# Storing finished output rows by row number while the last expert tile is still loading

## The chip, the cores and the metric

The program runs on one core of a Trainium2 chip. A core has a matrix engine (TensorE, PE in the profile), a vector engine (VectorE, DVE), an activation engine (ScalarE, ACT), a general engine (GpSimd, POOL) and a queue engine (SyncE, SP) that here only issues DMAs. Sixteen DMA engines move data between the chip's DRAM and the core's on-chip memory; the profile shows them by queue: q1 holds what SP issues, q10 what ACT issues, q0 what POOL issues. The metric is the time of one execution in microseconds on the device; less is better.

## The reference, cut to what matters

One decoder layer on 512 tokens of width 2048: three token mixers, then a mixture of experts, then a final normalisation. The change lies wholly in the last two. The last lines are

```python
# hier_moe: every token goes to 2 of 32 experts (top group, then top 2 in the group)
h = jax.nn.silu(lax.ragged_dot(xs, w_gate, sizes)) * lax.ragged_dot(xs, w_up, sizes)
y = lax.ragged_dot(h, w_down, sizes)
y = y * gates_flat[order][:, None]
out = jnp.zeros_like(xt).at[token_of].add(y)
# after it: residual add, then one last RMSNorm with gain final_norm_g
y = xf * lax.rsqrt(jnp.mean(xf * xf, axis=-1, keepdims=True) + EPS) * g
```

An output row is therefore finished once both experts of its token have been added. A row that no expert of the last tile touches is finished before the last tile is.

## The kernel before

**Tiles.** The tokens are sorted by expert and packed into 14 tiles of 128 places (`NTILE`, tiles 0 to 13; `LAST` is 13). The last tile holds four experts with 32 places each (`OWNERS`, `FOUR`). The kernel's second half is a loop over these tiles: a tile's rows are gathered from DRAM (`hs_d`) by POOL with an indirect DMA (L880), turned over by PE, multiplied by the gate and up weights (L1319), joined by ScalarE (silu) and VectorE, turned over again, and multiplied by the down weights. What comes out (`YSB`, one row for each place) is added to the rows of the residual `H0`, which holds all 512 rows as four blocks of 128 rows by 2048 columns. Adding is done by PE with a selection matrix `SEL` (POOL, L891): row t of a block picks the place that holds it, scaled by its gate; VectorE adds the product to `H0` (`combined`, L1774).

**Weights.** SP loads every expert's weights in order into eight slots and waits for a slot to be free before each load. For the last tile the gate and up weights come as four halves, each 4 x 2 MB, and the down weights as six pieces of columns (`DOWN_PIECES`: 512, 512 and four times 256 columns, each for four experts, issued at L744 and L746). Pieces 0 and 1 go into slots that the third half frees, pieces 2 to 5 into slots that the fourth frees. Nothing else is loaded after piece 5.

**The last tile.** `last_tile` on PE runs `first_products`, which goes through the four halves and calls `ahead(half)` before each: it fills PE's time while that half loads. In it stand what is left of adding tile 12 (`combine`) and, before the fourth half, the spreading of the final gain over the partitions. After the hidden values, six pieces follow (`y_part`, L1428: the down products of one piece; then `combine_part`, L1440: four selection products, one for each block of rows). ScalarE or VectorE copies each piece to `YSB` between the two. VectorE adds each product to `H0` (`add`), ScalarE squares it and sums (`square`), VectorE multiplies by the gain (`times_g`). After the last piece each block gets its sum, root and inverse (`sum_of`, `std`, `inverse_of`) and is scaled, blocks 0 and 2 on VectorE and 1 and 3 on ScalarE (`scaled`). SP stores each block in two halves (L750) and waits for all eight stores.

The order on every engine is written out by hand and held by semaphores; no scheduler moves anything.

Of the kernel before, what the change touches and what calls it, by code (L numbers as in the profile page):

```python
# [8 lines left out]
ALU = mybir.AluOpType  # L9
ACT = mybir.ActivationFunctionType  # L10
AX = mybir.AxisListType
# [90 lines left out]
def build(nc, d, out, cc):  # L102

    ctx = ExitStack()
    with ctx:
# [160 lines left out]
        FG, HG3, PART = XG[0], XT, TOT  # L266
# [173 lines left out]
        for at_, s in enumerate(steps):  # L440
# [50 lines left out]
        disc_act, disc_dve, disc_done = sem("disc_act"), sem("disc_dve"), sem("disc_done")  # L491
# [31 lines left out]
        g_done, out_dve, out_act, out_done = (  # L523
            sem("g_done"), sem("out_dve"), sem("out_act"), sem("out_done"))
# [7 lines left out]
        Y_BANK, Y_ACT = (4, 5, 6, 7, 4, 5), (True, False, True, False, True, False)  # L532
        Y_COPIES = [sum(Y_ACT[i] == Y_ACT[p] for i in range(p + 1)) for p in range(NPC)]

# [115 lines left out]
        def _(sp):  # L650
# [105 lines left out]
        def _(pool):  # L756
# [149 lines left out]
            with pool.If(flag > 0):  # L906
# [22 lines left out]
                pool.wait_ge(o_sel, NOV + 2)  # L929
            pool.wait_ge(sel_ready, LAST)  # L930
            selection(LAST)
# [3 lines left out]
        def _(pe):  # L935
# [58 lines left out]
            def do(s):  # L994
# [84 lines left out]
                elif kind == "ab":  # L1079
                    once(disc_done, 1)  # L1080
# [318 lines left out]
            def last_tile(n, parts):  # L1399

                def ahead(half):
                    for t in ((0, 1), (2,), (3,), ())[half]:
                        combine(n - 1, t)
                    if half == 3:
                        pe.wait_ge(fg_in, 16)
                        pe.wait_ge(comb_done, 16 * n + 1)
                        for q in range(4):
                            mm(B(4 + q, [(1, 512)]), F(C["ones"], P, 0, 1), F(FG + q * 512, 512, 0, 1), start=True,
                               stop=True).then_inc(fg_spread, 1)

# [3 lines left out]
                pe.wait_ge(fg_done, 4)  # L1414

                def y_part(p):
# [7 lines left out]
                    if p >= 4:  # L1424
                        pe.wait_ge(y_act if Y_ACT[p - 4] else y_dve, 2 * n + 1 + Y_COPIES[p - 4])
# [6 lines left out]
                def combine_part(p):  # L1432
                    lo, cols = PIECES[p][:2]
                    pe.wait_ge(y_act if Y_ACT[p] else y_dve, 2 * n + 1 + Y_COPIES[p])
                    if p == 0:
                        pe.wait_ge(sel_ready, n + 1)
                    for t in range(TB):
                        if p:
                            pe.wait_ge(comb_done, 16 * n + 4 * (p - 1) + t + 2)
                        mm(B(t, [(1, cols)]), F(SEL + t * P, P), F(YSB + lo, cols), start=True,  # L1440
                           stop=True).then_inc(comb_full, 1)

                for p in range(NPC):
                    y_part(p)
                    combine_part(p)
# [34 lines left out]
        def _(act):  # L1480
# [233 lines left out]
            def square(t, p):  # L1714
                lo, cols = PIECES[p][:2]
                act.wait_ge(comb_done, 16 * LAST + 4 * p + t + 2)
                A(F(SIL, cols), F(H0 + t * D + lo, cols), ACT.Square,
                  accum_out=F(PART + NPC * t + p, 1)).then_inc(squares_done, 1)
                act.wait_ge(squares_done, SQ0 + 4 * p + t + 1)

            def y_copy_last(p):
                lo, cols = PIECES[p][:2]
                act.wait_ge(y_full, 2 * LAST + p + 1)
                A(F(YSB + lo, cols), B(Y_BANK[p], [(1, cols)]), ACT.Copy).then_inc(y_act, 1)

            y_copy_last(0)
            A(F(SSQ, 1), F(EPSC, 1), ACT.Sqrt)
            for p in range(NPC - 1):
# [871 lines left out]
```

## Time and profile before

| | us |
|---|---|
| time before, median of 3 runs (lowest, highest) | 1947.87 (1946.85, 1950.14) |
| span of the profiled execution, first to last instruction | 1943.8 |
| median less that span: what lies around the instructions | 4.1 |
| last half of the gate and up weights: PE starts, ends | 1883.3, 1892.6 |
| first down product | 1894.9 |
| last down piece: PE starts | 1924.6 |
| first store of output issued | 1930.7 |

The profiled execution's own time is not given apart from its span; the median is 4.1 us longer than the span, and the two are taken to differ by that much.

The page of the profile gives busy shares over the whole span: PE 92%, VectorE 41%, ScalarE 13%, POOL 9%. From the twentieth slice on the DMA engines are 97 to 100% busy at some 425 GB/s: the expert loop runs at the pace of the weights. Only the last slice differs, with 7 tenths and 279 GB/s. What the change does all happens in the last 90 us, so the views are read for that stretch: the windows (busy time of each engine, clock and DMA share of a stretch), the timeline of one engine (start, duration, and in brackets the idle time before and what ended it), the DMA view of a window, and the chain that ended last.

### The profile page before, as it was taken

How to read it: one execution, taken by the hardware profiler on the slowest of the kernel's cores; microseconds unless marked ns; L12 is line 12 of the kernel's file. 1: busy time of each engine (PE TensorE's matmuls, PEld its weight loads, DVE VectorE, ACT ScalarE, POOL GpSimd, SP SyncE). 2: the span in 40 equal slices, each digit the busy share in tenths (PEclk: the TensorE clock that was granted, in tenths of full speed). 3: DMA queues.
4: the chain of work that ended last, by engine and by line, in shares of the span. 5: the costliest groups of instructions: out<-in, count | busy, mean ns of one | idle time of the engine just before them, and what ended most of it. 6: DMA issues, size and time to landing. Idle time of an engine off the chain costs nothing.

```text
span 1943.8 us, 30977 instructions
## 1 busy us (share of the span) xinstructions
PE 1792.7 (92%) x13019; PEld 1147.0 (59%) x13019; DVE 792.5 (41%) x1533; ACT 248.9 (13%) x588; POOL 173.5 (9%) x200
## 2 busy tenths in 40 slices
PE   6999999999999989999796679999999999999766
PEld 4888899889998879999642223332333333333222
DVE  7666684367467554333421112331222222222205
ACT  3012111200224431000210000000000000000004
POOL 1443342000000000000010000000000000000000
PEclk9999999999999999999898789999999999999988
DMA  6343333312121242422699999999999999999997
GB/s 220 98 139 88 99 88 90 101 63 66 52 85 55 71 170 66 173 67 66 275 378 425 426 427 425 426 426 425 422 425 422 423 425 426 425 424 423 416 413 279
DMA packets 68089, 506.12 MB, mean 260 GB/s; under 512 B 18824, under 2 KB 18972, under 8 KB 40872
## 3 DMA queue, kind: packets, MB, share of 16 engines
q1 hardware_dynamic: 50546, 480.40, 61.2%
q0 software_dynamic: 5008, 15.35, 2.4%
q10 hardware_dynamic: 12400, 8.36, 1.7%
q8 instruction: 109, 1.79, 0.4%
q14 instruction: 26, 0.21, 0.0%
HBM read 497.28 MB, written 12.99 MB: 263 GB/s over the span
## 4 chain that ended last, share of the span: by engine, by line
PE 69%; DMA 24%; DVE 3%; ACT 2%; issue 1%; SPq 1%; ACTq 0%; DVEq 0%
PE psum L986 20%; DMA arena<-in_moe_w_gate 17%; PE psum L1319 17%; PE psum L989 16%; PE psum L1278 5%; DMA arena<-in_moe_w_up 3%; DMA arena<-in_moe_w_down 3%; PE psum L1356 2%; PE psum L1144 2%; DVE arena L1774 1%; PE psum L1045 1%; PE psum L1428 1%; DVE arena L1777 1%; PE psum L1175 1%; PE psum L1440 1%
## 5 line engine op out<-in xcount | busy, mean ns | idle before, releaser
L1319 PE MATMUL psum<-arena 128*32 128x512 f32 x3584 | 417.4, 620 | 70.6 <-DMA arena<-in_moe_w_gate 38.0
L986 PE MATMUL psum<-arena 128*128 128x128 f32 x3584 | 410.7, 276 | 0.0
L986 PEld LDWEIGHTS psum<-arena 128*128 128x128 f32 x3584 | 405.3, 193 | 7.1 <-issue 6.4
L1774 DVE TENSOR_TENSOR arena<-psum,arena 128x512 f32<-128x512 f32 (+1 forms) x323 | 212.4, 674 | 403.2 <-PE psum L1278 374.3
L1319 PEld LDWEIGHTS psum<-arena 128*32 128x32 f32 x3584 | 119.4, 114 | 360.3 <-issue 349.6
L989 PE MATMUL psum<-arena 128*128 128x256 f32 x1456 | 322.4, 380 | 1.1 <-DVE arena L1774 1.1
L989 PEld LDWEIGHTS psum<-arena 128*128 128x128 f32 x1456 | 273.8, 190 | 38.7 <-issue 2.1
L1774 DVE TENSOR_TENSOR arena<-arena,psum 128x256 f32<-128x256 f32 (+2 forms) x172 | 75.1, 437 | 449.5 <-PE psum L986 215.6
L1774 DVE TENSOR_TENSOR arena<-arena 128x256 f32<-128x256 f32 (+17 forms) x474 | 191.2, 445 | 33.2 <-ACT arena L1486 25.3
L1356 PE MATMUL psum<-arena 128*32 128x512 f32 x1664 | 185.1, 603 | 17.9 <-DMA arena<-in_moe_w_down 17.9
L1278 PE MATMUL psum<-arena 128*128 128x512 f32 x416 | 192.1, 605 | 1.2 <-DVE arena L2417 1.2
L583 DVE TENSOR_TENSOR arena<-arena 128x1024 f32<-128x1024 f32 x116 | 149.0, 1285 | 3.2 <-DVE arena L1774 1.8
L1278 PEld LDWEIGHTS psum<-arena 128*128 128x128 f32 x416 | 74.9, 190 | 119.0 <-issue 119.0
L1356 PEld LDWEIGHTS psum<-arena 128*32 128x32 f32 x1664 | 54.2, 111 | 139.4 <-issue 138.4
L891 POOL TENSOR_SCALAR arena<-arena 128x512 f32<-128x512 f32 x14 | 29.1, 2080 | 788.1 <-PE psum L1278 787.7
L1551 ACT ACTIVATE arena<-psum 128x256 f32<-128x256 f32 x50 | 19.0, 381 | 291.8 <-PE psum L989 201.1
L1678 ACT ACTIVATE arena<-psum 128x512 f32<-128x512 f32 x14 | 8.4, 597 | 359.6 <-PE psum L1299 359.6
L1674 ACT ACTIVATE arena<-psum 128x512 f32<-128x512 f32 x14 | 8.4, 597 | 342.2 <-PE psum L1319 342.2
L2417 DVE COPY arena<-psum 128x512 f32<-128x512 f32 x13 | 9.0, 691 | 94.8 <-PE psum L1356 94.8
L2414 DVE COPY arena<-psum 128x512 f32<-128x512 f32 x13 | 9.0, 691 | 87.6 <-PE psum L1356 87.6
L1486 ACT ACTIVATE arena<-psum 128x512 f32<-128x512 f32 (+3 forms) x65 | 29.9, 484 | 92.4 <-PE psum L1133 25.1
L1634 ACT ACTIVATE arena<-arena 128x128 f32<-128x128 f32 (+3 forms) x48 | 26.6, 554 | 89.8 <-DVE arena L1777 89.7
(216 smaller groups left out, 1033.3 us busy)
## 6 DMA issues: line engine op xcount, KB each, us to landing
arena<-in_moe_w_gate SPq DMA_DIRECT2D x64, 2048.0 KB, 26.9
arena<-in_moe_w_up SPq DMA_DIRECT2D x64, 2048.0 KB, 25.0
arena<-in_moe_w_down SPq DMA_DIRECT2D x56, 2048.0 KB, 27.1
arena<-in_w_in SPq DMA_DIRECT2D x86, 512.0 KB, 4.6
arena<-in_w_out SPq DMA_DIRECT2D x32, 512.0 KB, 4.9
arena<-in_x SPq DMA_DIRECT2D x8, 1024.0 KB, 8.3
arena<-in_moe_w_down SPq DMA_DIRECT2D x8, 1024.0 KB, 18.2
arena<-in_moe_w_down SPq DMA_DIRECT2D x16, 512.0 KB, 12.1
```

The costliest lines, as they stand in the source:

```text
L583: e.tensor_tensor(F(o, BLK), F(a, BLK), F(b, BLK), ALU.subtract).then_inc(sums_ready, 1)
L891: g.tensor_scalar(F(SEL, S), F(IOTA, S), F(SELP, 1), F(SELP + 1, 1), ALU.is_equal, ALU.mult).then_inc(sel_ready, 1)
L986: last = mm(B(bank, [(1, P)], off=t * P), F(a + t * P, P), F(w + i * P, P), start=start and t == 0, stop=(i == KH - 1), skip_group_check=True)
L989: last = mm(B(bank, [(1, HB)]), F(w + i * P, P), F(a, HB), start=start, stop=(i == KH - 1), skip_group_check=True)
L1045: last = mm(B(bank, [(1, S)]), F(w + k * P, P), F(ZT + k * S, S), start=(k == 0), stop=(k == NB5 - 1))
L1144: last = mm(B(bank, [(1, P)], off=t * P), F(KT + h * S + t * P, P), F(QT + h * S + t * P, P), start=True, stop=True)
L1278: mm(B(4 + q, [(1, 512)]), F(SEL + t * P, P), F(YSB + q * 512, 512), start=True, stop=True).then_inc(comb_full, 1)
L1319: last = mm(B(bank, [(1, FE)], 32 * g, 32), F(xt + c * CAP + 32 * g, 32), F(SLOT[slot] + (c % 8) * FE, FE), start=(c == 0), stop=(c == KD ...
L1356: last = mm(B(4 + q, [(1, 512)], 32 * g, 32), F(HTE + m * CAP + 32 * g, 32), down_block(slot, m, q), start=(m == 0), stop=(m == FT2 - 1))
L1486: A(dst, B(bank, dims[0], *dims[1:]), func, **kw).then_inc(free[bank], 1)
L1634: last = A(x, x, ACT.Exp, bias=F(SM + (u % 2) * 8 + m, 1), accum_out=F(SM + (u % 2) * 8 + 2 + m, 1))
L1774: return v.tensor_tensor(o, a, b, op)
```

## The change

- **Early rows.** After tile 12 has been added, ScalarE squares and sums all of `H0` (four operations of 2048 columns), and VectorE scales the four blocks in place by the inverse root and the gain (four operations of 2048 columns).
- **Stores by row number.** POOL stores each block with an indirect DMA whose row numbers (`BIDX`) are the block's own rows, but out of bounds for rows that the last tile holds; those are not written. They are issued as soon as a block is scaled.
- **The last tile in its own rows.** PE gathers the raw `H0` rows of the last tile's 128 places into four PSUM banks with one-hot products (16 products of 512 columns, `ahead(3)`), before `H0` is scaled. A matrix `SAME` (places that hold the same token, scaled by their gate) takes the place of the four selection products: one product for a piece, added onto those banks. The norm is then worked out on 128 rows and not on 512, and one indirect DMA stores them by their token numbers.
- **Moved.** Tile 12's blocks 2 and 3 are both added before the second half, and the spreading of the gain moves from before the fourth half to before the third, with four turn-overs of the one-hot matrix (`OHS` to `OHT`) and one product for `SAME`.
- SP issues no store any more and waits for the five indirect ones. Down products use PSUM banks 0 and 1 in turn.
- `disc_done` is replaced by a count of `disc_dve`, far ahead in the program.

```diff
@@ sync
-            for t in range(TB):
-                for half in range(2):
-                    sp.wait_ge((out_dve, out_act)[t % 2], 3 * (t // 2) + 1 + 2 * half)
-                    sp.dma_start(DV(out, t * P * D + half * (D // 2), [(D, P), (1, D // 2)]),
-                                 F(H0 + t * D + half * (D // 2), D // 2)).then_inc(out_done, 16)
-            sp.wait_ge(out_done, 2 * 16 * TB)
+            sp.wait_ge(out_done, 16 * (TB + 1))
@@ gpsimd
-            selection(LAST)
+            pool.wait_ge(xT_full, 4 * LAST + 4)
+            g.tensor_copy(F(SELP, 1), TOKC[:, LAST:LAST + 1]).then_inc(sel_col, 1)
+            g.tensor_copy(F(SELP + 1, 1), GSLC[:, LAST:LAST + 1]).then_inc(sel_col, 1)
+            pool.wait_ge(sel_col, 2 * LAST + 2)
+            g.tensor_scalar(F(OHS, S), F(IOTA, S), F(SELP, 1), 1.0, ALU.is_equal, ALU.mult).then_inc(sel_ready, 1)
+            g.tensor_scalar(F(TOKD, P), F(IDENT, P), F(SELP, 1), 1.0, ALU.mult, ALU.mult).then_inc(sel_ready, 1)
+            def to_rows(src, idx):
+                g.indirect_dma_start(out=out[:, :], out_offset=bass.IndirectOffsetOnAxis(ap=idx, axis=0),
+                                     in_=F(src, D), in_offset=None, bounds_check=S - 1,
+                                     oob_is_err=False).then_inc(out_done, 16)
+            for t in range(TB):
+                pool.wait_ge(same_ready, t + 3)
+                to_rows(H0 + t * D, F(BIDX + t, 1).bitcast(U32))
+            pool.wait_ge(out_dve, 2)
+            pool.wait_ge(out_act, 1)
+            to_rows(HGS, TOKV[:, LAST:LAST + 1])
@@ tensor, last_tile
-                    for t in ((0, 1), (2,), (3,), ())[half]:
+                    for t in ((0, 1), (2, 3), (), ())[half]:
                         combine(n - 1, t)
-                    if half == 3:
+                    if half == 2:
+                        pe.wait_ge(sel_ready, n + 2)
+                        for t in range(TB):
+                            last = tr(B(0, [(1, P)], off=t * P), F(OHS + t * P, P), ident)
+                        last.then_inc(same_full, 1)
+                        mm(B(1, [(1, P)]), F(C["ones"], P), F(TOKD, P), start=True, stop=True).then_inc(same_full, 1)
                         ...
+                    elif half == 3:
+                        pe.wait_ge(same_ready, 1)
+                        for q in range(4):
+                            pe.wait_ge(fg_done, q + 1)
+                            for t in range(TB):
+                                last = mm(B(4 + q, [(1, 512)]), F(OHT + t * P, P), F(H0 + t * D + q * 512, 512),
+                                          start=(t == 0), stop=(t == TB - 1), skip_group_check=True)
+                        last.then_inc(same_full, 1)
-                def combine_part(p):
+                def same_part(p):
                     ...
+                    mm(final_bank(p), F(SAME, P), F(YSB + lo, cols), start=False, stop=True,
+                       skip_group_check=True).then_inc(comb_full, 1)
@@ scalar
+                for t in range(TB):
+                    A(F(YSB, D), F(H0 + t * D, D), ACT.Square, accum_out=F(SSQ + t, 1)).then_inc(squares_done, 1)
+                    act.wait_ge(squares_done, SQ0 + t + 1)
+                A(F(STD, TB), F(SSQ, TB), ACT.Sqrt, scale=1.0 / D, bias=F(EPSC, 1)).then_inc(h_std, 1)
             ...
+            for p, (lo, cols, *_) in enumerate(PIECES):
+                ...
+                act.wait_ge(comb_full, 16 * LAST + p + 2)
+                A(F(SIL, cols), final_bank(p), ACT.Square, accum_out=F(PART + p, 1)).then_inc(squares_done, 1)
+            ...
+            A(F(SSTD, 1), F(SSUM, 1), ACT.Sqrt, scale=1.0 / D, bias=F(EPSC, 1)).then_inc(h_std, 1)
+            ...
+            A(F(HGS + D // 2, lo - D // 2), F(HGS + D // 2, lo - D // 2), ACT.Copy, scale=F(SRST, 1)).then_inc(out_act, 1)
@@ vector
+            dve.wait_ge(h_std, 2)
+            v.reciprocal(F(RST, TB), F(STD, TB)).then_inc(h_rst, 1)
+            dve.wait_ge(h_rst, 2)
+            dve.wait_ge(fg_done, 4)
+            dve.wait_ge(same_full, 3)
+            for t in range(TB):
+                h = F(H0 + t * D, D)
+                v.scalar_tensor_tensor(h, h, F(RST + t, 1), F(FG, D), M, M).then_inc(same_ready, 1)
             hidden_dve(LAST, ends(last_parts())[1])
             ...
+                if p < LASTP:
+                    dve.wait_ge(squares_done, SQ0 + TB + p + 1)
+                    tt(F(HGS + lo, cols), final_bank(p), F(FG + lo, cols), M).then_inc(comb_done, 1)
             ...
+            ts(F(HGS, D // 2), F(HGS, D // 2), F(SRST, 1), None, M).then_inc(out_dve, 1)
+            v.scalar_tensor_tensor(F(HGS + lo, cols), final_bank(LASTP), F(SRST, 1), F(FG + lo, cols), M,
+                                   M).then_inc(out_dve, 1)
```

On TensorE, from the last half's products to the second down piece, the program before reads as follows (L1319 up products, L1299 turn-overs of the hidden values, L1428 down products, L1440 selection products):

```order
L1319 MATMUL psum<-arena 32x512 [waits slot_in4,slot_in1,slot_in6,slot_in3]
L1319 MATMUL psum<-arena 32x512 x31
L1299 MATMUL psum<-arena 128x128 [waits h_done]
L1299 MATMUL psum<-arena 128x128 x3
L1428 MATMUL psum<-arena 32x512 [waits slot_in7,slot_in2,slot_in5,slot_in0,fg_done,hT_done]
L1428 MATMUL psum<-arena 32x512 x15
L1440 MATMUL psum<-arena 128x512 [waits sel_ready,y_act]
L1440 MATMUL psum<-arena 128x512 x3
L1428 MATMUL psum<-arena 32x512 [waits tail_in1]
L1428 MATMUL psum<-arena 32x512 x15
```

The same place in the changed program, from the last of the gathering products (new L1440) on; L1339, L1319, L1458 and L1469 are up products, turn-overs, down products and `SAME` products:

```order
L1440 MATMUL psum<-arena 128x512 [waits fg_done]
L1440 MATMUL psum<-arena 128x512 x3
L1339 MATMUL psum<-arena 32x512 [waits slot_in4,slot_in1,slot_in6,slot_in3]
L1339 MATMUL psum<-arena 32x512 x31
L1319 MATMUL psum<-arena 128x128 [waits h_done]
L1319 MATMUL psum<-arena 128x128 x3
L1458 MATMUL psum<-arena 32x512 [waits slot_in2,slot_in7,slot_in0,slot_in5,hT_done]
L1458 MATMUL psum<-arena 32x512 x15
L1469 MATMUL psum<-arena 128x512 [waits same_ready,y_act]
L1458 MATMUL psum<-arena 32x512 [waits tail_in1]
```

Sixteen gathering products now stand ahead of the last half, and after each down piece one product stands where four stood.

On VectorE, from the adding of tile 12 on, the program before reads as follows (the second row is the hidden product of the last tile, the third and fourth are the additions of piece 0, the last its multiplications by the gain):

```order
L1774 TENSOR_TENSOR arena<-psum,arena 128x512 [waits comb_full] x16
L1774 TENSOR_TENSOR arena<-arena,psum 128x512 [waits silu_done,slot_used1]
L1774 TENSOR_TENSOR arena<-psum,arena 128x512 [waits comb_full,fg_done]
L1774 TENSOR_TENSOR arena<-psum,arena 128x512 [waits comb_full] x3
L1774 TENSOR_TENSOR arena<-arena 128x512 [waits squares_done] x4
```

The same place in the changed program (L2471 scales the early rows, the L1778 behind it is the hidden product):

```order
L1778 TENSOR_TENSOR arena<-psum,arena 128x512 [waits comb_full] x16
L2457 COPY arena<-psum 128x512 [waits same_full]
L1781 TENSOR_SCALAR arena<-psum,arena 128x128 [waits same_full]
L2461 TENSOR_REDUCE arena<-arena 128x4 [waits same_ready]
L2462 SCALAR_TENSOR_TENSOR arena<-arena 128x4 [waits dve_step]
L2463 CAST arena<-arena 128x4 [waits dve_step]
L2465 RECIPROCAL arena<-arena 128x4 [waits h_std,dve_step]
L2471 SCALAR_TENSOR_TENSOR arena<-arena 128x2048 [waits same_full,fg_done,h_rst]
L2471 SCALAR_TENSOR_TENSOR arena<-arena 128x2048 x3
L1778 TENSOR_TENSOR arena<-arena,psum 128x512 [waits silu_done,slot_used1]
```

The hidden product of the last tile waits behind the four scalings, and these wait for the last gathering product.

## Rows read from the trace of the kernel before

**Rows 1.** Span and mean granted TensorE clock of the core.
```profile
core 0: 1943.8 us, clock 0.969
```

**Rows 2.** Windows of 1889 to 1923 us: stretch, length, busy by engine, PEclk, DMA share, GB/s.
```profile
1889.00:1903.00 14.00, 11.63 (x80) 3.75 (x72) 2.81 (x5) 4.24 (x9) 0.00 (x0) 1.00 1.01 406
1903.00:1916.00 13.00, 11.41 (x88) 4.95 (x92) 10.36 (x18) 5.58 (x17) 0.00 (x0) 1.00 1.02 404
1916.00:1923.00 7.00, 5.89 (x74) 3.47 (x67) 5.10 (x14) 3.49 (x14) 0.00 (x0) 1.00 0.35 140
```

**Rows 3.** Timeline of SP, last weight load and last store; start, duration.
```profile
1908.07 0.93 SPq L746 DMA_DIRECT2D arena<-in_moe_w_down  x1
...
1938.70 1.13 SPq L750 DMA_DIRECT2D out<-arena  x1
```

**Rows 4.** DMA view of 1908.0 to 1908.2: that load; last number us to landing.
```profile
arena<-in_moe_w_down SPq DMA_DIRECT2D x1, 512.0 KB, 15.4
```

**Rows 5.** Timelines of PE and ACT, last tile; start, duration, records, idle before.
```profile
1863.71 8.87 PE L1319 MATMUL psum<-arena 128*32 128x512 f32 x64 [7.54 <-DMA arena<-in_moe_w_up]
1872.52 3.70 PE L1408 MATMUL psum<-arena 1*128 1x512 f32 x8
...
1873.67 0.60 ACT L1710 ACTIVATE arena<-psum 128x512 f32<-128x512 f32 x1 [20.39 <-PE psum L1408]
...
1883.34 9.30 PE L1319 MATMUL psum<-arena 128*32 128x512 f32 x64 [7.13 <-DMA arena<-in_moe_w_up]
1894.86 3.64 PE L1428 MATMUL psum<-arena 128*32 128x512 f32 x32 [0.69 <-ACT arena L1678]
...
1924.55 1.93 PE L1428 MATMUL psum<-arena 128*32 128x256 f32 x32
```

**Rows 6.** The chain that ended last, from the last piece; start, duration, engine and line.
```profile
1926.55 0.44 DVE arena L2469
...
1927.03 0.71 PE psum L1440 x2
...
1928.35 0.32 ACT arena L1717
...
1928.68 0.19 ACT arena L1717
...
1929.43 0.30 ACT arena L1736
...
1929.76 0.17 DVE arena L2492
```

**Rows 7.** Groups of instructions, 1889 to 1944: busy us, mean ns of one.
```profile
L1777 DVE TENSOR_SCALAR arena<-arena 128x1024 f32<-128x1024 f32 (+1 forms) x4 | 2.6, 684 | 0.1
L2500 DVE SCALAR_TENSOR_TENSOR arena<-arena 128x256 f32<-128x256 f32 x2 | 1.0, 480 | 0.0
```

**Rows 8.** Timeline of VectorE: four multiplications by the gain, 2048 columns in all.
```profile
1903.56 2.49 DVE L1774 TENSOR_TENSOR arena<-arena 128x512 f32<-128x512 f32 x4
```

**Rows 9.** Timeline of POOL: the gather for the last tile.
```profile
1681.04 1.09 POOL L880 DMA_INDIRECT arena<-hs_rows,arena  x1 [0.87 <-POOL arena L877]
```

**Rows 10.** DMA view of 1681.0 to 1684.7: queues with packets, MB, share; that gather.
```profile
q1 hardware_dynamic: 109, 1.59, 101.1%
...
arena<-hs_rows,arena POOLq DMA_INDIRECT x1, 12.7
```

**Rows 11.** DMA view of 1684.7 to 1692.3: packets, MB, share of each queue.
```profile
q1 hardware_dynamic: 203, 2.95, 92.2%
q0 software_dynamic: 142, 0.25, 8.6%
```

**Rows 12.** DMA view of the page: sizes in KB, median us to landing.
```profile
arena<-y_scratch POOLq DMA_DIRECT2D x5, 256.0 KB, 3.0
```

**Rows 13.** DMA view of 1939.2 to 1944: the last store of the output.
```profile
out<-arena SPq DMA_DIRECT2D x1, 512.0 KB, 4.7
```

**Rows 14.** DMA view of 988 to 991, weights beside stores of hidden rows (q10).
```profile
DMA packets 108, 1.28 MB, mean 426 GB/s; under 512 B 1, under 2 KB 1, under 8 KB 1
```

More of the change, by code:

```diff
@@ L265, in build @@
         SEL, SELP = SIL + 4 * CAP, SIL + 4 * CAP + S
-        FG, HG3, PART = XG[0], XT, TOT
+        FG, HGS, PART = XG[0], XT, TOT
+        OHS, OHT, SAME, TOKD, BIDX = XG[1], XG[1] + S, XG[1] + 2 * S, XG[1] + 2 * S + P, XG[1] + 2 * S + 2 * P
+        SSUM, SSTD, SRST, HASL = SM + 1, SM + 2, SM + 3, SM + 4
         assert RO2 == RO1 + 128
@@ L1079, in do @@
                 elif kind == "ab":
-                    once(disc_done, 1)
+                    once(disc_dve, 3)
                     for i, r in enumerate((10, 11, 14, 15)):
@@ L1435, in combine_part @@
                     if p == 0:
[L1436 to L1441, printed above, removed]
+                        pe.wait_ge(same_ready, 2)
+                    if lo % 512:
+                        pe.wait_ge(comb_done, 16 * n + p + 1)
+                    mm(final_bank(p), F(SAME, P), F(YSB + lo, cols), start=False, stop=True,
+                       skip_group_check=True).then_inc(comb_full, 1)
                 for p in range(NPC):
                     y_part(p)
-                    combine_part(p)
+                    same_part(p)
             expert_tile(0, 0, 0, fixed_parts(), THREE_ONE, True)
@@ L1721, in y_copy_last @@
[L1721 to L1728, printed above, removed]
-                if p and Y_ACT[p]:
-                    y_copy_last(p)
-                for t in range(TB):
-                    square(t, p)
-            def std(t):
-                act.wait_ge(squares_sum, t + 2)
-                A(F(STD + t, 1), F(SSQ + t, 1), ACT.Sqrt, scale=1.0 / D, bias=F(EPSC, 1)).then_inc(h_std, 1)
@@ L1746, in _ @@
[L1746 to L1755 removed]
+            for p, (lo, cols, *_) in enumerate(PIECES):
+                if Y_ACT[p]:
+                    act.wait_ge(y_full, 2 * LAST + p + 1)
+                    A(F(YSB + lo, cols), B(Y_BANK[p], [(1, cols)]), ACT.Copy).then_inc(y_act, 1)
+                act.wait_ge(comb_full, 16 * LAST + p + 2)
+                A(F(SIL, cols), final_bank(p), ACT.Square, accum_out=F(PART + p, 1)).then_inc(squares_done, 1)
+                act.wait_ge(squares_done, SQ0 + TB + p + 1)
@@ L2466, in y_copy @@
-            def y_copy(p):
-                lo, cols = PIECES[p][:2]
-                dve.wait_ge(y_full, 2 * LAST + p + 1)
-                v.tensor_copy(F(YSB + lo, cols), B(Y_BANK[p], [(1, cols)])).then_inc(y_dve, 1)
-            dve.wait_ge(fg_done, 4)
-            for p in range(LASTP):
-                if not Y_ACT[p]:
-                    y_copy(p)
-                for t in range(TB):
-                    add(t, p)
-                if p < LASTP - 1:
-                    for t in range(TB):
-                        times_g(t, p)
@@ L2508, in _ @@
-            settle()
-            add(0, LASTP)
-            add(1, LASTP)
-            sum_of(0)
-            last_g(1)
-            add(2, LASTP)
-            inverse_of(0)
-            scaled(0)
-            sum_of(1)
-            add(3, LASTP)
-            inverse_of(1)
-            sum_of(2)
-            last_g(3)
-            inverse_of(2)
-            sum_of(3)
-            inverse_of(3)
-            scaled(2)
+            dve.wait_ge(same_full, 1)
+            v.tensor_copy(F(OHT, S), B(0, [(1, S)])).then_inc(same_ready, 1)
@@ new lines, in _ @@
+            dve.wait_ge(same_full, 2)
+            ts(F(SAME, P), B(1, [(1, P)]), F(SELP, 1), F(SELP + 1, 1), ALU.is_equal, M).then_inc(same_ready, 1)
+            dve.wait_ge(same_ready, 2)
+            settle(v.tensor_reduce(F(HASL, TB), V(OHT, [(P, TB), (1, P)]), AX.X, ALU.max))
+            settle(v.scalar_tensor_tensor(F(HASL, TB), F(HASL, TB), SENT, F(C["tok"], TB), M, AD))
+            settle(v.tensor_copy(F(BIDX, TB).bitcast(U32), F(HASL, TB)))
+            dve.wait_ge(h_std, 2)
+            v.reciprocal(F(RST, TB), F(STD, TB)).then_inc(h_rst, 1)
```

86 lines of the change are left out of this document (22 added, 64 removed).

## The prediction

> **What bounds the kernel now.** I read the windows of the last weights first. From 1889 to 1916 us the DMA share is 1.01 and 1.02, at 406 and 404 GB/s; from 1916 to 1923 it falls to 0.35 [rows 2]. So up to the last weights the stretch belongs to the DMA engines. A share of 0.35 over 7 us means that some of the sixteen engines work longer than the others, and that weights land until the slowest is through: the last load is issued at 1908.07 [rows 3] and lands 15.4 us later [rows 4], at 1923.5. TensorE is next: its clock is 1.00 all along [rows 2], its first down product starts at 1894.86 and the last piece at 1924.55, 1.1 us after its weights are there [rows 5]. TensorE's and the DMA's ends thus nearly coincide. The chain then runs through copy, selection product, square, root and scaling to the last store, issued at 1938.70 [rows 3] and landed 4.7 us later [rows 13], at 1943.4; the span ends at 1943.8 [rows 1], 0.4 us behind.
>
> From the landing of the last weights to the end it is 20.3 us. The change attacks these, and in return puts stores into the stretch where the DMA engines have no idle time. That exchange is the whole question.
>
> **Change, part 1: the early stores among the weights.** The gather for the last tile shows how many rows that tile holds: in its stretch queue q0 moved 0.25 MB [rows 11], and a row is 8 KB, so some 30 rows. The early stores leave these out and move 482 rows, 3.95 MB. They start when VectorE has scaled a block. The sixteen gathering products begin when the third half is done, at 1872.5; four products of 512 columns take 3.70 us there [rows 5], sixteen 14.7, to 1887.2. Each scaling has 2048 columns, which four multiplications of 512 did in 2.49 us [rows 8]; with fewer starts I take 2.25. The blocks are ready at 1889.5, 1891.7, 1894.0 and 1896.2.
>
> Are the stores served at once, or behind the weights? The gather put its 142 packets through in 7.6 us while q1 held 92% [rows 11]: q0 gets its turn beside a full q1. Four stores of 1 MB, issued by 1896.3 and moving from 3.7 us later (below), are through well before 1916. So all 3.95 MB pass ahead of the last weights, on engines that were never idle up to there. Stores and loads share one rate, they don't add: stores of hidden rows beside weights moved 426 GB/s together [rows 14]. At 426 GB/s the 3.95 MB take 9.3 us, at the 406 of this stretch [rows 2] 9.7. I take 9.4, since rows of 8 KB resemble the former. A lower bound: between 1916 and 1923 0.65 of the engines' time lies idle, 4.5 us; if the weights were dealt out so that this is used, the shift is 4.9. I don't take it, because the engine that ends last has its own share of the stores, and that isn't lent. The last weights land at 1923.5 + 9.4 = 1932.9.
>
> **Part 2: TensorE and VectorE ahead of the pieces.** The last half starts at 1887.2 instead of 1883.3 [rows 5]. Its 9.30 us held a slow start after 7.13 us of waiting; without that wait it should take 7 to 9.3, and ends at 1894.2 to 1896.5. The loads of pieces 2 to 5 wait for it, 2 to 4 us longer than before, while pieces 0 and 1 (8.4 MB issued, 20 us at the rate of rows 2) still fill the queue to past 1903. The hidden product on VectorE now stands behind the four scalings, until 1896.3; the first down product starts at about 1898.5 instead of 1894.86. From there TensorE alone would need, for pieces 0 and 1, 3.64 [rows 5] + 0.75 for the copy + 0.93 for one product, and for the other four 1.93 + 0.55 + 0.50 each: 10.6 + 11.9, to 1921. It is 12 us ahead of weights that land at 1932.9, so all of part 2 costs nothing; if the weights came unshifted, at 1923.5, it would still be hidden. For the same reason the 18 selection products that go gain nothing by themselves; only the last piece's count, in part 3. The four squares and the copies of the gain lie where ScalarE waited 20.39 us [rows 5]; a copy of 512 columns took 0.60 there, so a square of 2048 takes at most 2.4, and all four some 10. On TensorE the gain's spreading (3.70) changes places with the addition of block 3, as long as itself; only the turn-overs and the product for `SAME` are new before the third half, some 1 us, against 7.54 us of waiting [rows 5]. I cost all of it at nothing.
>
> **Part 3: from the last weights to the last store issued.** The same chain, one piece, one block [rows 6]: start of the piece to start of its copy 2.00, copy and hand-over 0.48 (next product at 1927.03), first product 0.80 with hand-over; then, without the addition to the residual, square 0.32 and its accumulator 0.19, with hand-overs 0.54; a reduction, taken as long as the reciprocal, 0.21; root 0.34; reciprocal 0.21; scaling 1024 columns 0.68 and 256 from PSUM 0.48 [rows 7], ScalarE's 768 columns beside them. Sum 5.7. The scaled rows stand at 1932.9 + 0.1 + 5.7 = 1938.7. Before, the last scaling and store issue were 15.2 us behind the weights; now 5.8. This is the gain: 9.4 us, and it happens to equal the shift of part 1.
>
> **Part 4: the last store.** Before it was a plain store of 512 KB by SP, 4.7 us with one before it in the queue [rows 13]. Now it is an indirect one by POOL. The gather is the nearest row: 0.87 us between the instruction ahead and its start [rows 9], 12.7 us from issue to landing, and no packet of q0 until 3.7 us after the issue [rows 10]; all packets lie within the next 7.6 us [rows 11], so 1.4 us are left for completion. These 3.7 + 1.4 = 5.1 are fixed. Without weights in the way the data take what the fullest engine has: eight rows of 8 KB at 426/16 GB/s, 2.5 us, even if the other engines are nearly empty. Landing after 7.6 us. The gap ahead I take as 0.6, between 0 and 0.87. Lower bound for the landing: POOL's plain loads of 256 KB landed in 3.0 [rows 12]. Upper: the gather's 12.7.
>
> The Trainium skill ("DMA: Bandwidth & Descriptors", section "Anatomy of one DMA — SWDGE (gpsimd) path") has another price for a DMA issued by POOL: about 2.0 us fixed plus the bytes at 436 GB/s. By it the last store, 0.25 MB, would take 2.6 us and the sum would come out 5.0 us lower. The gather's rows disagree: 3.7 us pass before the first packet alone. I go by the rows.
>
> **Sum.** 1938.7 + 0.6 + 7.6 + 0.4 = 1947.3 against 1943.8: 3.5 us longer. On the median of the runs shown that is 1947.87 + 3.5 = 1951.4, +0.18%. About 0.2% (3.9 us) is what a measurement of this kernel can tell from no change; the forecast is a loss just inside it. It comes from small terms: shift +9.4, chain -9.4, last store +3.5 (8.2 with its gap against 4.7).
>
> **Rivals.**
>
> *Slower: the mixed stretch runs below its rate.* Writes of rows to DRAM beside reads may cost more than 9.4 us for 3.95 MB. For it: the rate of this stretch is 405 and not 426 although the share is full [rows 2]. Against: rows 14. The outcome passes +0.2% once the shift is over 9.8 us, that is, when the stores run under 403 GB/s. At 340 GB/s it is 11.6 us and the time 1951.4 + 2.2 = 1953.6. An engine with no row left out carries 32 rows, 0.26 MB, at 405/16 GB/s 10.4 us: 1952.4.
>
> *Same, a little lower: idle engine time absorbs stores.* Shift 4.9 in place of 9.4: 1946.9. For it the 0.35 of rows 2, against it that the slowest engine carries its own part.
>
> *Faster: the last store is cheap as well.* If it lands in 3.0 us as POOL's plain loads do [rows 12], alone 1951.4 - 4.6 = 1946.8, no change that can be told; with the rival before it 1942.3.
>
> *Faster: the early stores wait.* If POOL's stores got little of the engines until the weights are through, the weights would land at 1923.5 and the last piece be ready at 1929.3; the stores would drain from 1923 to 1933 behind them and the last land at about 1936.5: 1943.8 - 6.9, a time of 1941.0. Then the change would do only half of what it says, and win by it. Against it: rows 11.
>
> **How the numbers follow.** The forecast's case (shift 9.3 to 9.8, last store 7 to 8 us) 0.42, most of it within 0.2%; slower by a lower rate, by a fuller engine or by a longer last store 0.38; absorbed or cheap store alone 0.10; both, or waiting stores 0.10. The sum lies near the bound, so I count 0.05 of the first case as slower: slower 0.43, same 0.47, faster 0.10. The likeliest is 1951.4, by itself 1950 to 1952. The range for 8 in 10: down to 1946.5, the absorbed case, and up to 1956, which is the 340 GB/s case with 2 us more for the last store.
>
> **What would show it.** Right: DMA share near 1 until about 1925 and the last weight landing at 1932 to 1934; TensorE waiting for DMA before most pieces; the last POOL store issued near 1939 to 1940 and landing some 8 us later; early stores done by 1916. Wrong in part 1 if the last weights land before 1930 or after 1935; in part 2 if TensorE starts the last piece more than 0.3 us after its weights; in part 4 if the last store takes under 6 or over 9 us.

## The result and the profile after

| | before | changed |
|---|---|---|
| median of 10 runs each, us | 1947.9 | 1951.43 |
| lowest, highest | 1945.7, 1950.14 | 1950.4, 1954.39 |
| span of the profiled execution | 1943.8 | 1949.2 |

The ratio of changed to before is 1.0019, 95% interval 1.0011 to 1.0027: 3.5 us longer. A second series of the same kernel, beside three of the experiments, gave 1951.94 against 1947.48, ratio 1.0023 (1.0014 to 1.0032), with a span of 1947.7. The two profiled executions differ by 5.4 us and not 3.5; 1.3 us of that difference is a delay in front of the change (TensorE ends the third half at 1873.8 and not 1872.5), which the second series' profile doesn't have: there TensorE ends it at 1872.3 and the span is 3.9 us longer. Nor do 4.1 us lie around the instructions, as was assumed for the kernel before: in every run on record with both numbers, a time is 1.8 to 3.1 us longer than its span, so the profiled execution before was a fast one. So all stretches below are counted from the end of the third half's products.

The windows of the changed kernel (stretch, length, busy time of PE, PEld, DVE, ACT and POOL, PEclk, DMA share, GB/s) answer to [rows 2]:

```profile
1889.00:1903.00 14.00, 10.38 (x84) 3.01 (x80) 8.64 (x5) 0.60 (x1) 7.08 (x4) 0.88 1.01 420
1903.00:1916.00 13.00, 6.47 (x38) 1.41 (x30) 0.69 (x1) 1.29 (x3) 0.00 (x0) 0.74 1.01 419
1916.00:1920.00 4.00, 3.18 (x30) 0.86 (x26) 0.69 (x1) 0.32 (x1) 0.00 (x0) 0.99 1.03 410
1920.00:1924.00 4.00, 2.14 (x30) 0.91 (x22) 1.12 (x2) 1.22 (x5) 0.00 (x0) 1.00 1.03 407
1924.00:1926.00 2.00, 1.70 (x32) 0.94 (x32) 0.00 (x0) 0.00 (x0) 0.00 (x0) 1.00 1.03 412
1926.00:1928.00 2.00, 0.93 (x9) 0.30 (x2) 0.42 (x1) 0.43 (x2) 0.00 (x0) 1.00 0.83 334
1928.00:1930.00 2.00, 0.61 (x11) 0.33 (x15) 0.42 (x1) 0.05 (x1) 0.00 (x0) 0.93 0.40 162
```

The full share reaches to 1926 where in the kernel before it ended at about 1916, at the same rate or a little more. Its TensorE timeline, from the gathering products (L1440) on, answers to [rows 5]; in brackets stands the idle time before and what ended it:

```profile
1873.76 14.00 PE L1440 MATMUL psum<-arena 128*128 128x512 f32 x32
1887.69 7.07 PE L1339 MATMUL psum<-arena 128*32 128x512 f32 x64
1897.70 0.66 PE L1319 MATMUL psum<-arena 128*128 128x128 f32 x4 [2.94 <-DVE arena L1778]
1899.04 5.29 PE L1458 MATMUL psum<-arena 128*32 128x512 f32 x32 [0.69 <-ACT arena L1707]
...
1911.99 5.64 PE L1458 MATMUL psum<-arena 128*32 128x512 f32 x32 [5.80 <-DMA arena<-in_moe_w_down]
...
1929.39 3.38 PE L1458 MATMUL psum<-arena 128*32 128x256 f32 x32 [1.92 <-DMA arena<-in_moe_w_down]
...
1934.46 1.93 PE L1458 MATMUL psum<-arena 128*32 128x256 f32 x32 [0.45 <-DMA arena<-in_moe_w_down]
```

Ahead of most pieces TensorE now waits for DMA, and it starts the last piece as the weights land; the kernel before started it 1.1 us after its weights. The end of the program stands in two views: POOL's timeline, and the source view of the closing instructions (minimum, median and maximum duration in ns, first and last start). A DRAIN is the instruction that closes an engine's program; SP's COMPARE_BRANCH is the first thing it does after its last wait, so its start tells when the last awaited transfer landed.

```profile
1891.14 2.31 POOL L942 DMA_INDIRECT out<-arena  x1 [85.99 <-DVE arena L2471]
1893.76 1.87 POOL L942 DMA_INDIRECT out<-arena  x1 [0.30 <-issue]
1895.94 1.94 POOL L942 DMA_INDIRECT out<-arena  x1 [0.30 <-issue]
1898.18 0.96 POOL L942 DMA_INDIRECT out<-arena  x1 [0.30 <-issue]
1940.97 0.96 POOL L942 DMA_INDIRECT out<-arena  x1 [41.83 <-DVE arena L2488]
```

```profile
L105 POOLq DRAIN  x1: 8208/8208/8208, 1940.8 to 1940.8; - x1
L105 SPq COMPARE_BRANCH  x1: 38/38/38, 1945.4 to 1945.4; - x1
```

The last store landed 4.4 us after its issue, at 1945.4, and SP, which waits for it, goes on at that moment. The program isn't over: POOL's closing DRAIN lasts 8.2 us and ends at 1949.0, 3.6 us behind the landing. What it follows, the experiments show. In the kernel before, the same instruction lay far from the end, and SP's last wait set it:

```profile
L105 POOLq DRAIN  x1: 8752/8752/8752, 1856.3 to 1856.3; - x1
...
L105 SPq COMPARE_BRANCH  x1: 37/37/37, 1943.4 to 1943.4; - x1
```

The difference of the two spans, in stretches:

| stretch | before | changed | difference |
|---|---|---|---|
| to the end of the third half | 1872.5 | 1873.8 | +1.3 |
| from there to the landing of the last weights | 51.0 (1923.5) | 60.6 (1934.4) | +9.6 |
| from there to the last scaled row or last store issue | 15.2 (1938.7) | 5.8 (1940.2) | -9.4 |
| from there to the end | 5.1 (1943.8) | 9.0 (1949.2) | +3.9 |

### The profile page after: what moved, and what is told of

Read it like the earlier page. It is cut to its first block, busy times and chain, and to the rows that moved or that the text cites. A ratio compares the mean times of both kernels' runs of the same rounds, so it can differ in the third digit from the quotient of the medians.

```text
span 1949.2 us, 30885 instructions
## 1 busy us (share of the span) xinstructions
PE 1801.3 (92%) x13021; PEld 1146.5 (59%) x13021; DVE 781.7 (40%) x1492; ACT 241.8 (12%) x552; POOL 181.7 (9%) x206
## 4 chain that ended last, share of the span: by engine, by line
PE 69%; DMA 22%; DVE 4%; SPq 2%; issue 1%; ACT 1%; POOLq 0%; DVEq 0%; POOL 0%; ACTq 0%
PE psum L1006 20%; PE psum L1339 16%; DMA arena<-in_moe_w_gate 16%; PE psum L1009 16%; PE psum L1298 5%; DMA arena<-in_moe_w_up 3%; PE psum L1376 3%; DMA arena<-in_moe_w_down 2%; PE psum L1164 2%; DVE arena L1778 2%; PE psum L1065 1%; SPq L753 1%; PE psum L1278 1%; PE psum L1440 1%; DMA arena<-hs_rows,arena 1%
## 5 line engine op out<-in xcount | busy, mean ns | idle before, releaser
L1339 PE MATMUL psum<-arena 128*32 128x512 f32 x3584 | 415.9, 618 | 56.8 <-DMA arena<-in_moe_w_gate 37.8
L1778 DVE TENSOR_TENSOR arena<-psum,arena 128x512 f32<-128x512 f32 x304 | 202.8, 684 | 394.8 <-PE psum L1298 356.5
L1339 PEld LDWEIGHTS psum<-arena 128*32 128x32 f32 x3584 | 118.4, 113 | 345.7 <-issue 327.7
L1778 DVE TENSOR_TENSOR arena<-arena,psum 128x256 f32<-128x256 f32 (+2 forms) x172 | 75.1, 437 | 411.9 <-PE psum L1006 215.6
L1778 DVE TENSOR_TENSOR arena<-arena 128x128 f32<-128x128 f32 (+17 forms) x452 | 181.0, 442 | 33.0 <-ACT arena L1515 25.1
```

The source lines that it names most:

```text
L1339: last = mm(B(bank, [(1, FE)], 32 * g, 32), F(xt + c * CAP + 32 * g, 32), F(SLOT[slot] + (c % 8) * FE, FE), start=(c == 0), stop=(c == KD ...
L1778: return v.tensor_tensor(o, a, b, op)
```

## Experiments

Ten kernels ran on the chip, each in five rounds beside the kernel before. A time is compared through its ratio to the kernel before in the same series; the intervals are about 0.09% to each side, 1.7 us, and 0.13% for the last kernel. Where a kernel stores fewer rows, SP's last wait counts fewer stores; that line isn't shown everywhere. Five kernels (no early stores, half of them, SP's plain stores with and without the wait for piece 4, the copy in place of the last store) leave rows of the output unwritten and serve only to tell causes apart.

### No early stores

```diff
-            for t in range(TB):
-                pool.wait_ge(same_ready, t + 3)
-                to_rows(H0 + t * D, F(BIDX + t, 1).bitcast(U32))
```

> Leaves out the four early stores, so that only the last tile's rows are written; all else as in the changed kernel. Theory A (stores and weights share one DMA rate): the last weights land 9.7 us earlier counted from the end of the third half's products, about 51 us behind them and not 60.6; time 1951.4 - 9.7 = 1941.7. Rival B (the later start of TensorE and VectorE delays the weights): they land 2 us earlier at most, time 1949 to 1951.

1943.49 us against 1947.65, ratio 0.9978 (0.9969 to 0.9987). Its TensorE timeline, third half's end and last piece:

```profile
1872.85 14.00 PE L1437 MATMUL psum<-arena 128*128 128x512 f32 x32
1886.78 7.07 PE L1336 MATMUL psum<-arena 128*32 128x512 f32 x64
...
1923.80 1.93 PE L1455 MATMUL psum<-arena 128*32 128x256 f32 x32 [0.41 <-DMA arena<-in_moe_w_down]
```

The last weights land at 1923.8, 50.9 us behind the third half, as in the kernel before. All that TensorE and VectorE do later in the changed kernel is still in it (sixteen gathering products, the last half at 1886.8), so none of this delays the weights: the 9.7 us come from the stores, and rival B falls. The time is 1.8 us above the 1941.7 expected: the medians give 8 us for the stores, the landings in the profiles 9.7.

### Half of the early stores

```diff
-            for t in range(TB):
+            for t in range(2):
                 pool.wait_ge(same_ready, t + 3)
```

> Only blocks 0 and 1 are stored early, blocks 2 and 3 not at all; all else as in the changed kernel. Theory A (each early byte delays the weights by its time at the common rate): half the bytes give half the shift, last weights 55.8 us behind the end of the third half's products, between 50.9 without early stores and 60.6 with all four; time midway between the two, about 1947. Rival F (idle engine time at the end absorbs the first few us of stores, about 4.5 us): the shift is near 0 to 1 us for two blocks, time 1943.5 to 1944.5.

1947.84 against 1947.48, ratio 1.0002 (0.9993 to 1.0011): in time midway, 4.1 us below the changed kernel of the same series (1951.94) and 4.4 above the one without early stores (of the other series). In the trace the weights land 54.5 us behind the third half (1874.6), a shift of 3.6 us and not 4.9:

```profile
1929.15 1.93 PE L1458 MATMUL psum<-arena 128*32 128x256 f32 x32 [0.56 <-DMA arena<-in_moe_w_down]
```

The engine that ends last counts, and its share of the rows in each block isn't shown; that may be why half the stores gave a third of the shift. Rival F (the first few us are free) fails: 3.6 us isn't near 0 to 1.

### Early stores after the last weights

```diff
+            pool.wait_ge(tail_in[5], 4 * 16)
             for t in range(TB):
                 pool.wait_ge(same_ready, t + 3)
```

> The early stores wait until the last piece of weights has landed (one more wait on POOL ahead of them). Theory A: weights land as in the kernel before, the stores' 9.5 us run beside the last chain (5.8 us) and beside what POOL needs at the end; the end is the last weights + 5.8 + 2 + 8.2 = 16 us behind the weights, against 20.3 before: 1943.5. Rival C (the bytes cost the same wherever they stand): 1951, since the same bytes then stand behind the weights. Rival B: 1951, nothing changes.

1946.64 against 1947.65, ratio 0.9994 (0.9985 to 1.0003). Slower than expected by 3 us, but some 5 us faster than the changed kernel, which rules out rival C. The weights land 51.4 us behind the third half, 0.5 more than without early stores although no early store had begun: half a microsecond is the scatter of these landings, and the shift in the changed kernel is 9.2 to 9.7 us. What I had missed stands in the closing instructions:

```profile
L105 POOLq DRAIN  x1: 11662/11662/11662, 1932.5 to 1932.5; - x1
L105 SPq COMPARE_BRANCH  x1: 38/38/38, 1940.6 to 1940.6; - x1
```

The stores land at 1940.6, because they started only at 1926, and POOL's DRAIN ends 3.6 us behind that, at 1944.2. Its windows show what lay idle before:

```profile
1920.00:1924.00 4.00, 3.31 (x32) 1.39 (x32) 0.00 (x0) 0.36 (x1) 0.00 (x0) 0.62 0.25 99
1924.00:1928.00 4.00, 2.63 (x34) 1.24 (x34) 0.42 (x1) 0.50 (x3) 1.59 (x2) 1.00 0.10 39
```

### Early stores after piece 4, and after piece 3

```diff
-            pool.wait_ge(tail_in[5], 4 * 16)
+            pool.wait_ge(tail_in[4], 4 * 16)
```

> The early stores wait for piece 4 of the weights instead of piece 5. In the run that waited for piece 5 the DMA engines were busy 0.25 and 0.10 of 1920 to 1928, and POOL's DRAIN ended 3.6 us behind the landing of the stores at 1940.6. Theory A+D: stores start 5 us earlier in idle time, land before the floor of last POOL instruction + 7 us, and the end falls by 3 us against that run, to 1943.5; the weights land up to 1 us later. Rival F: the weights still land unshifted. Rival G (stores delay the slowest engine by their full time wherever they start before its end): weights 3 us or more later and no gain.

1942.97 against 1947.48, ratio 0.9978 (0.9969 to 0.9987): 4.5 us faster than the kernel before, 9.0 faster than the changed kernel in the same series. All outputs are stored. TensorE's last piece, POOL's timeline and the windows:

```profile
1925.12 1.93 PE L1459 MATMUL psum<-arena 128*32 128x256 f32 x32 [0.47 <-DMA arena<-in_moe_w_down]
```

```profile
1920.87 1.07 POOL L942 DMA_INDIRECT out<-arena  x1 [115.55 <-DMA arena<-in_moe_w_down]
...
1931.62 0.96 POOL L942 DMA_INDIRECT out<-arena  x1 [5.86 <-DVE arena L2489]
```

```profile
1920.00:1924.00 4.00, 3.39 (x33) 1.44 (x33) 0.00 (x0) 0.38 (x1) 2.52 (x3) 0.63 0.56 228
1924.00:1928.00 4.00, 2.98 (x36) 1.48 (x36) 0.85 (x2) 0.47 (x2) 1.46 (x2) 1.00 0.99 402
1928.00:1932.00 4.00, 0.30 (x2) 0.00 (x0) 1.47 (x4) 1.70 (x4) 0.38 (x1) 0.72 1.00 412
1932.00:1936.00 4.00, 0.00 (x0) 0.00 (x0) 0.00 (x0) 0.00 (x0) 0.59 (x1) 0.50 0.30 117
```

The stores fill 1923 to 1933. The last weights land at 1925.1, 51.4 us behind the third half, 0.4 later than without early stores and no later than in the kernel that waits for piece 5, so rival G fails; 0.4 us is too little to tell theory A from rival F here. The stores' first packets came between 1922.3 and 1922.6, 2.8 us ahead of that landing, and until 1923.5 the weights kept a share of 0.23 to 0.27 of the engines, as without stores; why the stores took so little from them isn't shown. All stores have landed at 1936.1, the DRAIN ends at 1939.6, 7.0 us behind POOL's last instruction.

The same with one piece less to wait for:

```diff
-            pool.wait_ge(tail_in[5], 4 * 16)
+            pool.wait_ge(tail_in[3], 4 * 16)
```

> The early stores wait for piece 3. They then start at about 1918 to 1919, when four engines still carry weights for 5 us. Theory A: on these the stores take half the turns, weights 2 to 5 us later, time 1945 to 1948, above the kernel that waits for piece 4. Rival F: idle engine time takes them, weights unshifted, time 1943 or less.

1952.64 against 1947.48, ratio 1.0026 (1.0017 to 1.0036), 9.7 us slower than the wait for piece 4. Counted from the third half the stores are issued 5.0 us earlier, and the last weights now pay for nearly all of them, as the last piece on TensorE shows:

```profile
1932.06 3.35 PE L1459 MATMUL psum<-arena 128*32 128x256 f32 x32 [8.98 <-DMA arena<-in_moe_w_down]
```

The last weights land at 1932.0, 59.9 us behind the third half (1872.2), a shift of 9.0. That is nearly the full price, though the mean share of the engines in the stretch was far under 1 (0.20 from 1928 to 1932). The piece itself took 3.35 us at the low clock and not 1.93. Rival F fails, and my bound for theory A (2 to 5 us later) was too low. One part of that is plain: the first packets of the stores came between 1916 and 1917, 44 us behind the third half, so that weights which land at 51 without stores had some 7 us to go, and not 5. The other is how two queues share an engine. The DMA view of 1918 to 1922 (packets, MB, share of each queue; q0 is POOL's, q1 the weights'):

```profile
q0 software_dynamic: 214, 1.49, 88.6%
q1 hardware_dynamic: 57, 0.20, 12.2%
```

In the kernel that waits for piece 5 the last weights alone moved some 28 packets in each us, a share of about 0.25; here they got half of that, 57 packets in 4 us. A packet of q0 carried 7.0 KB on the average and one of q1 3.5, so turns in equal number would favour the stores; that this is the reason isn't shown.

### What the last store costs: another queue, and a copy in its place

The last rows by SP to a scratch tensor, so that the output lacks them:

```diff
-            pool.wait_ge(out_dve, 2)
-            pool.wait_ge(out_act, 1)
-            to_rows(HGS, TOKV[:, LAST:LAST + 1])
@@ sync
+            for half in range(2):
+                sp.wait_ge(out_dve, 1 + half)
+                ...
+                sp.dma_start(DV(hs_d, half * (D // 2), [(D, P), (1, D // 2)]),
+                             F(HGS + half * (D // 2), D // 2)).then_inc(fg_in, 16)
+            sp.wait_ge(fg_in, 48)
+            sp.wait_ge(out_done, 16 * TB)
```

> The last tile's rows are stored by SP with two plain stores to a scratch tensor, so the output lacks them; early stores unchanged. Theory D (POOL's closing DRAIN, 8.2 us behind its last instruction, sets the end, and not the landing of 4.4 us): the end comes with SP's landing, 3 to 4.7 us behind the issue at about 1940.3 of the changed kernel's span, 1944.5 against 1949.2: time 1951.4 - 4.5 = 1946.9. Rival E (the indirect store's own landing sets the end): gain at most 1 us, time 1950.4 or more.

1946.94 against 1947.65, ratio 1.0000 (0.9991 to 1.0009). The last weights are still late, at 1933.1, and the span ends 9.7 us behind them (1942.8) instead of 14.8. Theory D forecast a gain of 4.5 us; the span gives 5.1 and the ratios 3.7, both more than the 1 us of rival E. SP's wait ends the span; POOL's DRAIN ended at 1917.5, 3.5 us behind the landing of its last early store:

```profile
L105 POOLq DRAIN  x1: 21081/21081/21081, 1896.4 to 1896.4; - x1
...
L105 SPq COMPARE_BRANCH  x1: 38/38/38, 1942.4 to 1942.4; - x1
```

In the next kernel POOL's last act is a copy of one column in place of the store, after the same waits; SP waits for the copy, and the last tile's rows aren't stored:

```diff
-            to_rows(HGS, TOKV[:, LAST:LAST + 1])
+            g.tensor_copy(F(SELP + 1, 1), F(SELP, 1)).then_inc(sel_col, 1)
```

> In place of the last store POOL copies one column after the same waits; the last tile's rows are not stored. Theory D: the DRAIN behind it takes 8 us just so, and the time stays within 1 us of 1951.4 less the store's own issue (up to 1 us). Rival E: without the store nothing lands late and the time falls to 1951.4 - 8 = 1943.

1950.23 against 1947.65, ratio 1.0018 (1.0009 to 1.0027), where the changed kernel has 1.0019. Nothing lands at the end of this program, and it is as long:

```profile
1940.16 0.19 POOL L952 COPY arena<-arena 128x1 f32<-128x1 f32 x1 [41.09 <-DVE arena L2489]
```

```profile
L105 POOLq DRAIN  x1: 7173/7173/7173, 1940.1 to 1940.1; - x1
L105 SPq COMPARE_BRANCH  x1: 37/37/37, 1940.4 to 1940.4; - x1
```

SP is free at 1940.4; POOL's DRAIN ends at 1947.3, 7.0 us behind the copy, with nothing of its own in flight. Rival E falls.

### The same copy in the kernel before, and the best place with SP's store

```diff
             selection(LAST)
+            pool.wait_ge(out_dve, 6)
+            pool.wait_ge(out_act, 6)
+            pool.wait_ge(sel_ready, LAST + 1)
+            g.tensor_copy(F(SELP + 1, 1), F(SELP, 1)).then_inc(sel_col, 1)
```

> The kernel before with one more instruction: POOL copies one column once the last scaling of the output is done (about 1938.5 of its span). All outputs are stored. Theory D (a DRAIN of POOL ends 7.0 us behind its last instruction, whatever that is): the span ends at 1938.7 + 7 = 1945.7 in place of 1943.8, time 1947.5 + 1.9 = 1949.4. Rival H (only an indirect DMA makes the DRAIN long at the end): no change, 1947.5.

1949.78 against 1946.72, ratio 1.0016 (1.0007 to 1.0025), 3.1 us slower for a copy of 0.19 us that nobody waits for:

```profile
1939.49 0.19 POOL L935 COPY arena<-arena 128x1 f32<-128x1 f32 x1 [79.82 <-ACT arena L1748]
```

```profile
L105 POOLq DRAIN  x1: 6830/6830/6830, 1939.5 to 1939.5; - x1
L105 SPq COMPARE_BRANCH  x1: 38/38/38, 1944.3 to 1944.3; - x1
```

The DRAIN ends at 1946.3, 2.0 us behind SP and 6.6 behind the end of the copy; rival H falls. The other 1.1 us lie within the interval. The last kernel takes the early stores after piece 4 and SP's plain stores to scratch for the last rows:

```diff
+            pool.wait_ge(tail_in[4], 4 * 16)
             for t in range(TB):
                 pool.wait_ge(same_ready, t + 3)
             ...
```

The rest of it is as in the kernel with SP's plain stores.

> The kernel whose early stores wait for piece 4, with the last tile's rows stored by SP in two plain stores of 512 KB to a scratch tensor (the output lacks these rows). Theory D: the end comes with SP's landing; POOL's own stores carry until about 1935 in both, so 1 MB of SP's stores beside 1 to 2 MB of POOL's lands at about 1936.5 of that kernel's span, 3 us below its 1939.9: time 1940. Rival: the end is set by bytes, not by POOL's DRAIN: no gain, 1943.

1939.88 against 1946.72, ratio 0.9962 (0.9948 to 0.9975). The time is as expected, the end isn't: SP's stores have landed at 1936.9, but POOL's DRAIN ends at 1938.0 and still comes last, 12 us behind the end of POOL's last instruction (1925.7). The last packets of its early stores lie between 1934.0 and 1934.5, so this is the closing that follows a late landing:

```profile
L105 POOLq DRAIN  x1: 15693/15693/15693, 1922.3 to 1922.3; - x1
L105 SPq COMPARE_BRANCH  x1: 38/38/38, 1936.9 to 1936.9; - x1
```

So moving the last store to SP shortens POOL's closing and doesn't take it off the end. Against the kernel that waits for piece 4 the span of the profile is 1.7 us shorter; the ratios differ by 3.1 us, with intervals of about that size together. It isn't a version to use: SP's plain store doesn't put rows where their numbers say.

The changed kernel again, in the series of the kernels with half of the early stores and with the waits for piece 4 and piece 3 (its result stands in the section on the result):

> The changed kernel itself, beside the others on the same chip: 1951.4, 0.2% above the kernel before.

## Why the prediction was right

The prediction was 1951.4 (1946.5 to 1956), the result 1951.43. That the two agree to a tenth is luck: the landing of the last store was put 3.2 us too dear, and 3.6 us of POOL's closing behind it weren't in the sum at all. Its steps fared as follows.

**Part 1, right.** The shift of the weights was put at 9.4 us and measured at 9.6 against the kernel before, and without the early stores at 0. Blocks were expected ready between 1889.5 and 1896.2, and POOL issued from 1891.1 to 1898.2, 1.3 us of it the delay ahead of the change. The last early store landed 17.0 us after its issue, at 1915.2, ahead of the last weights as argued. Stores and weights moved 420 and 419 GB/s together, so the rival of a lower mixed rate didn't come in. The bound of idle engine time was rightly not taken for all four stores: the kernel that waits for piece 3 shows the last weights paying 9.0 us while most engines stand idle. For half of the stores the shift, 3.6 us, is less than their own time.

**Part 2, right in what it costs, not in how.** The last half started at 1887.7 and took 7.07 us, the first down product came at 1899.0; both starts are within 0.6 us. The 12 us of slack were there, but not as a lead, since every piece waits for its own weights: TensorE waited 5.80, 1.59, 1.92 and 0.45 us for DMA, and two pieces behind such a wait ran at the low clock, 5.64 and 3.38 us in place of 3.64 and 1.93. The first piece, behind 2.94 us of waiting for the hidden product on VectorE, took 5.29. Still, it started the last piece as its weights landed, in the changed kernel and in the one without early stores.

**Part 3, right.** 5.7 us from the last weights to the scaled rows, measured 5.8; the gain of 9.4 us came as worked out.

**Part 4, right in its sum alone.** I put 0.6 + 7.6 + 0.4 = 8.6 us behind the scaled rows, and it was 9.0. But the store doesn't take 7.6 us: it landed in 4.4, with its first packets 1.4 to 1.7 us after the issue and not 3.7. The gather's rows [rows 9 to 11] were taken under a full load, and both its start and its completion were dearer; that the load is the reason is argued, not shown. What ends the program is the closing of POOL, which the prediction doesn't name: 3.6 us more. By the prediction's own sign (a last store under 6 us) this part is wrong. The steps that failed are "I go by the rows" for the landing, and the 0.4 us put behind it, which belong to an end set by SP; the row that would have told it is POOL's DRAIN of 8.75 us in the trace before, far from the end and harmless there. The Trainium skill's price ("DMA: Bandwidth & Descriptors", section "Anatomy of one DMA — SWDGE (gpsimd) path"), about 2.0 us plus the bytes at 436 GB/s and so an estimate of 2.6 us for 0.25 MB, is under the 4.4 measured, though nearer than mine. By it alone the forecast would have been 5.0 us too low, as it knows nothing of the closing either.

The rival "slower" was the same story with a dearer shift; the rival "the early stores wait" describes, with its weights unshifted, what a wait for piece 4 brought about on purpose. It put the last landing at about 1936.5, and there it was 1936.1; the time was 1943.0 and not 1941.0, since POOL's closing came 3.5 us behind.

## What to carry to other kernels

A transfer put beside a saturated stream isn't hidden; it delays the stream's last byte by up to its own time, and the mean share of the engines doesn't show by how much. Here 3.95 MB cost 9.7 us beside the weights and at most 0.4 us once they wait until most engines have run dry, about 4 us ahead of the last landing; issued 5 us earlier than that they cost 9.0: one wait turned a loss of 0.2% into a gain of 0.2%. And before an engine gets the last word of a program, look up how long its closing DRAIN takes in the trace: on POOL here some 7 us behind its last instruction, and 3.5 us behind the landing of its last transfer if that is later.

## What the runs showed of the hardware

- **POOL closes slowly.** Its DRAIN ended 6.6 to 7.1 us after the end of its last instruction in every run where nothing of its own was still in flight late (7.0 behind a copy, 6.6 behind a copy in the kernel before, 7.1 behind the last store of the changed kernel), and 3.5 to 3.6 us after the landing of its last DMA where that is later (1944.2 behind 1940.6). Behind a last store of 4.4 us both come to the same; the kernels that end with a copy show the first alone. The closings of TensorE, VectorE and ScalarE took 0.7 to 2.4 us.
- **Indirect DMA alone and under load.** From issue to landing 4.4 to 4.5 us on idle engines with some 30 rows; 10.8 to 17.0 us for the four of the changed kernel, which carry up to 128 rows each and followed one another beside weights.
- **VectorE stretches POOL's issue.** Three of the early stores took 2.31, 1.87 and 1.94 us on POOL while VectorE scaled blocks from two operands in on-chip memory, and 0.96 to 1.07 otherwise (the fourth store, all five in the kernel that waits for piece 4, and all five in the one that waits for piece 3, whose first are issued beside a full stream, too). The Trainium skill ("SBUF — State Buffer", section "Who interferes with whom") says that a VectorE instruction with two SBUF inputs contends with a GpSimd instruction that reads SBUF, and the trace agrees. VectorE didn't pay: its four scalings took 9.14 us with and without.
- **Waiting costs clock.** In the changed kernel TensorE stood idle for 2.94 us (for VectorE), 5.80 and 1.92 us (for weights) shortly ahead of three down pieces. The granted clock then read 0.50 from 1899 to 1902, from 1912 to 1916 and from 1930 to 1933, and these pieces ran 5.29, 5.64 and 3.38 us where they take 3.64 or 1.93 at a clock of 1.00. The piece behind a wait of 1.59 us ran at full clock.
